# Last token block of a dense feed-forward stage: the down products of part 9 moved behind part 10 and accumulated with its own, tile by tile

## What is computed

```python
h = _layer_norm(x) * (1 + sc2) + sh2
a = jax.nn.silu(jnp.einsum('bsd,df->bsf', h, w_gate[l])) * jnp.einsum('bsd,df->bsf', h, w_up[l])
ffn = jnp.einsum('bsf,fd->bsd', a, w_down[l])
x = _layer_norm(ALPHA * x + (1 + g2) * ffn) * ln2_g[l] + ln2_b[l]
```

## Time and profile before

| what | value |
|---|---|
| median of 3 runs | 3033.78 us |
| span of the profiled execution | 3027.8 us |
| TensorE busy | 2900.4 us (96%) |
| VectorE busy | 2137.8 us (71%) |
| ScalarE busy | 1275.6 us (42%) |
| GpSimd busy | 1405.7 us (46%) |
| last matmul group ends | about 3005.2 us |
| last VectorE instruction begins | 3023.43 us |

### The profile page before, as it was taken

The page is one execution under the profiler, slowest core; times in us unless marked ns, Lnnn a source line. Parts: engine busy times, 40 slices in busy tenths (PEclk is TensorE's granted clock), DMA queues, the critical chain, the costliest instruction groups (busy, mean ns, idle before and its releaser), DMA issues.

```text
span 3027.8 us, 39376 instructions
## 1 busy us (share of the span) xinstructions
PE 2900.4 (96%) x14244; PEld 2438.3 (81%) x14244; DVE 2137.8 (71%) x3095; ACT 1275.6 (42%) x2287; POOL 1405.7 (46%) x1109
## 2 busy tenths in 40 slices
PE   7999998999999998999799999999999999999996
PEld 3888886666666656888789999989999989999995
DVE  5666665988888865566666666677777667777767
ACT  3111113777777764456533223343333333333334
POOL 0233321011111125568745545585677466676655
PEclk9999999999999998999999999999999999999998
DMA  7344337021312106366432122242332233322322
GB/s 260 120 140 133 121 121 191 28 70 58 84 58 72 50 22 213 121 214 212 170 125 70 56 84 70 84 157 77 119 112 82 86 109 132 118 86 103 112 70 91
DMA packets 194061, 333.02 MB, mean 110 GB/s; under 512 B 15366, under 2 KB 102599, under 8 KB 193866
## 3 DMA queue, kind: packets, MB, share of 16 engines
q1 hardware_dynamic: 193868, 330.49, 33.9%
HBM read 250.72 MB, written 79.71 MB: 109 GB/s over the span
## 4 chain that ended last, share of the span: by engine, by line
PE 51%; POOL 4%; DVE 3%; DVEq 1%; issue 1%; DMA 1%; POOLq 1%; ACT 1%; SPq 0%; ACTq 0%
PE tail_bank L2298 9%; PE tail_bank L2300 9%; PE tail_bank L2299 9%; PE tail_bank L2322 6%; PE tail_bank L2323 6%; PE tail_bank L2324 5%; PE tail_bank L2237 1%; PE tail_bank L2236 1%; PE tail_bank L2235 1%; POOL tail_rounded L2031 1%; POOL tail_rounded L2039 1%; DMA tail_plain<-scr_h_d 1%; PE tail_bank L2184 0%; POOL tail_plain L2027 0%; PE tail_bank L2176 0%
## 5 line engine op out<-in xcount | busy, mean ns | idle before, releaser
L2031 POOL TENSOR_TENSOR tail_rounded<-tail_plain,tail_rounded 128x512 fp32r<-128x512 f32 x462 | 648.4, 1425 | 491.0 <-ACT tail_rounded L1815 490.5
L2298 PE MATMUL tail_bank<-tail_rounded 128*128 128x384 f32 x1848 | 621.8, 336 | 18.9 <-POOL tail_rounded L2039 11.3
L2299 PE MATMUL tail_bank<-tail_rounded 128*128 128x384 f32 x1848 | 620.8, 336 | 0.0
L2300 PE MATMUL tail_bank<-tail_rounded 128*128 128x384 f32 x1848 | 620.6, 336 | 0.0
L2467 DVE TENSOR_TENSOR tail_plain<-tail_plain,tail_bank 128x384 f32<-128x384 f32 x462 | 247.9, 549 | 264.1 <-PE tail_bank L2300 198.5
L1815 ACT ACTIVATE tail_rounded<-tail_plain 128x512 fp32r<-128x512 f32 x462 | 271.4, 621 | 368.5 <-DVE tail_plain L2445 177.4
L2298 PEld LDWEIGHTS tail_bank<-tail_rounded 128*128 128x128 f32 x1848 | 348.6, 189 | 23.2 <-issue 17.0
L2299 PEld LDWEIGHTS tail_bank<-tail_rounded 128*128 128x128 f32 x1848 | 348.7, 189 | 1.3
L2300 PEld LDWEIGHTS tail_bank<-tail_rounded 128*128 128x128 f32 x1848 | 348.8, 189 | 0.0
L1154 DVE TENSOR_REDUCE att_peak<-att_sc 128x1 f32<-128x1024 f32 x256 | 312.7, 1222 | 42.5 <-PE att_sc L966 35.9
L2322 PE MATMUL tail_bank<-tail_rounded 128*128 128x512 f32 x792 | 311.8, 394 | 21.3 <-issue 7.1
(11 more groups left out here) (286 smaller groups left out, 5142.7 us busy)
## 6 DMA issues: line engine op xcount, KB each, us to landing
tail_plain<-in_w_gu SPq DMA_DIRECT2D x132, 512.0 KB, 4.9
keep_ahead<-in_w_dn SPq DMA_DIRECT2D x66, 512.0 KB, 6.6
proj_ada<-in_w_ada SPq DMA_DIRECT2D x16, 1024.0 KB, 6.8
held_w_hi<-scr_qs_d SPq DMA_DIRECT2D x128, 128.0 KB, 2.9
scr_h_d<-tail_plain SPq DMA_DIRECT2D x63, 256.0 KB, 4.5
tail_plain<-scr_h_d SPq DMA_DIRECT2D x45, 256.0 KB, 4.3
proj_x_in<-in_x SPq DMA_DIRECT2D x18, 512.0 KB, 6.4
scr_att_d<-held_w_hi SPq DMA_DIRECT2D x36, 256.0 KB, 2.9
```

The source lines that it names most:

```text
L2031: nc.gpsimd.tensor_tensor(w_lo[:, j, :], operand(F, j), w_hi[:, j, :].bitcast(F32), ALU.subtract).then_inc(wlo_done, 1)
L2298: nc.tensor.matmul(dst, w_hi[:, j, cols], h_hi[j][:, k, :], start=(k == 0), stop=False)
L2299: nc.tensor.matmul(dst, w_hi[:, j, cols], h_lo[j][:, k, :], start=False, stop=False)
L2300: m = nc.tensor.matmul(dst, w_lo[:, j, cols], h_hi[j][:, k, :], start=False, stop=(k == 3))
```

## The change

For the last part only (`END` = 32):

- TensorE: `down(31)` no longer stands between the two phases of part 32. Behind the second phase comes `last_two_downs`: the products of part 31 for the first four banks, then those of part 32 on top of them in the same banks; from the fifth bank on the products of both parts for one bank follow each other. VectorE reads each bank once, 12 reads instead of 24.
- Buffers: the activation and the down weights of part 32 go to the space of `h_hi[0]`, `h_lo[0]` and of `h_hi[1]`, `h_hi[2]`, `h_lo[1]`, `h_lo[2]`, since those of part 31 are still needed. So ScalarE's `split_down` and `split_a` wait for products of the second phase.
- `gate_sums` of tiles 0 to 3 goes from GpSimd to VectorE, between the two phases' takes, of tiles 4 and 5 it stays on GpSimd, but behind the four `split_a`.
- VectorE: `residual(0)` and `residual(1)` move ahead of and behind `take_u` of the second phase; both `split_down` move behind the first `multiply`; `residual(2)` comes after the last `multiply`, and `residual(n + 3)` and `finish(n - 1)` come inside the last loop.

```diff
+        last_a_hi, last_a_lo = (tile.rearrange("p (i c) t -> p i c t", c=2) for tile in (h_hi[0], h_lo[0]))
+        last_dn_hi, last_dn_lo = cut(11264, D, "i", i=2), cut(20480, D, "i", i=2)
...
             def split_down(G, i):
                 act.wait_ge(dnraw_landed[i], 16 * (G + 1))
-                if G:
+                if G == END:
+                    act.wait_ge(prod_done, OPERANDS * (2 * G + 1) + 3)
+                elif G:
                     act.wait_ge(dn_done, BANKS * G)
...
                 for j in range(OPERANDS):
+                    if j == 3 and is_last(b, part):
+                        split_down(G, 0)
+                        split_down(G, 1)
...
                 elif is_last(b, part):
-                    for n in range(TILES):
-                        gate_sums(G - 1, n)
                     for n in range(4):
                         split_a(G, n)
+                    for n in range(TILES - PT, TILES):
+                        gate_sums(n)
...
+            def last_two_downs():
+
+                for m_ in range(BANKS):
+                    if m_ == 0:
+                        pe.wait_ge(dnlo_done, 2 * END)
+                        pe.wait_ge(alo_done, 4 * END)
+                        for ahead_ in range(4):
+                            pe.wait_ge(added, BANKS * (END - 2) + BANKS - 3 + ahead_)
+                            down_products(END - 1, ahead_, True, False)
+                        pe.wait_ge(dnlo_done, 2 * END + 2)
+                        pe.wait_ge(alo_done, 4 * END + 2)
+                    if m_ == 4:
+                        pe.wait_ge(alo_done, 4 * END + 4)
+                    if m_ >= 4:
+                        pe.wait_ge(added, BANKS * (END - 1) + m_ - 3)
+                        down_products(END - 1, m_, True, False)
+                    down_products(END, m_, False, True).then_inc(dn_done, 1)
+
             def step(b, part, G):
                 phase(b, part, 2 * G)
                 if G == 0:
                     turn(NT - 2)
-                if part:
+                if part and G < END:
                     down(G - 1)
                 phase(b, part, 2 * G + 1)
-                if closes(part):
+                if G == END:
+                    last_two_downs()
+                elif closes(part):
                     down(G)
...
-                if part:
+                if is_last(b, part):
+                    last_sum_w(F + 1)
+                    for n in range(TILES - PT):
+                        gate_sums(total[:, DOWN_ORDER[n], :])
+                elif part:
                     down(b, part - 1, G - 1, beside_gate)
 
+                if is_last(b, part):
+                    residual(0)
                 take_u(F + 1, up)
                 if is_last(b, part):
-                    residual(2)
+                    residual(1)
                 elif G:
                     sums_w(F + 2)
-                if G:
+                if G and not is_last(b, part):
                     split_down(G, 0)
                 take_v(F + 1, up)
-                if closes(part):
+                if closes(part) and not is_last(b, part):
                     split_down(G, 1)
                 take_c11(F + 1, up)
                 multiply(G, 0)
                 if is_last(b, part):
-                    residual(3)
+                    split_down(G, 0)
+                    split_down(G, 1)
                 take_c21(F + 1, up)
...
             parts(step)
-            gate_last(0)
-            add_last(0)
-            gate_last(1)
-            residual(4)
-            add_last(1)
-            for n in range(2, TILES):
+            residual(2)
+            for n in range(TILES):
                 gate_last(n)
-                if n == 2:
-                    residual(5)
                 add_last(n)
-            for n in range(TILES):
-                finish(n)
+                if n < TILES - 3:
+                    residual(n + 3)
+                if n:
+                    finish(n - 1)
+            finish(TILES - 1)
```

More of the change, by code:

```diff
@@ L1453, in fourier_to_end, with a_of, dn_of @@
         LAST = NT - TILES
+        END = PARTS * BLOCKS - 1
+        def a_of(G):
+            return (last_a_hi, last_a_lo) if G == END else (a_hi, a_lo)
+        def dn_of(G):
+            return (last_dn_hi, last_dn_lo) if G == END else (dn_hi, dn_lo)
         def last_gate(n, half):
@@ L1853, in split_a @@
                 act.wait_ge(mult_done, 4 * G + n + 1)
-                if n == 0 and G:
+                if n == 0 and G == END:
+                    act.wait_ge(prod_done, OPERANDS * (2 * G + 1) + 1)
+                elif n == 0 and G:
                     act.wait_ge(dn_done, BANKS * G)
-                nc.scalar.activation(a_hi[:, i, c, :], sil[:, i, c, :], ACT.Copy).then_inc(ahi_done, 1)
+                nc.scalar.activation(a_of(G)[0][:, i, c, :], sil[:, i, c, :], ACT.Copy).then_inc(ahi_done, 1)
             def normalise(N, tile, at):
@@ L2043, in split_a @@
                 pool.wait_ge(ahi_done, 4 * G + n + 1)
-                nc.gpsimd.tensor_tensor(a_lo[:, i, c, :], sil[:, i, c, :], a_hi[:, i, c, :].bitcast(F32), ALU.subtract).then_inc(alo_done, 1)
+                hi, lo = a_of(G)
+                nc.gpsimd.tensor_tensor(lo[:, i, c, :], sil[:, i, c, :], hi[:, i, c, :].bitcast(F32), ALU.subtract).then_inc(alo_done, 1)
             def rstd(N, at):
@@ L2050, in rstd, with gate_sums @@
                 nc.gpsimd.tensor_tensor(at[:, 5:6], at[:, 4:5], at[:, 3:4], ALU.mult).then_inc(rstd_done, 1)
-            def gate_sums(G, n):
-                pool.wait_ge(added, BANKS * G + 2 * n + 2)
+            def gate_sums(n):
+                pool.wait_ge(added, BANKS * (END - 2) + 2 * n + 2)
                 if n == TILES - PT:
                     pool.wait_ge(row2_landed, 80)
[L2057 to L2060, removed]
+                for half in range(2):
+                    tile = total[:, DOWN_ORDER[n], half * 512:(half + 1) * 512]
+                    ins = nc.gpsimd.tensor_tensor(tile, tile, last_gate(n, half), ALU.mult)
                 ins.then_inc(gated, 1)
@@ L2317, in down @@
                         pe.wait_ge(added, BANKS * G + m_ - 3)
[L2318 to L2324, removed]
@@ L2325, in down, with down_products @@
-                    m.then_inc(dn_done, 1)
+                    down_products(G, m_, True, True).then_inc(dn_done, 1)
+            def down_products(G, m_, first, final):
+                pos, half = divmod(m_, 2)
+                q, c = divmod(DOWN_ORDER[pos], 2)
+                hi, lo = a_of(G)
+                w_hi, w_lo = dn_of(G)
+                dst = dn(m_)
+                tokens = slice(q * P, (q + 1) * P)
+                cols = slice(half * 512, (half + 1) * 512)
+                for i in range(2):
+                    nc.tensor.matmul(dst, hi[:, i, c, tokens], w_hi[:, i, cols], start=(first and i == 0), stop=False)
+                    nc.tensor.matmul(dst, hi[:, i, c, tokens], w_lo[:, i, cols], start=False, stop=False)
+                    m = nc.tensor.matmul(dst, lo[:, i, c, tokens], w_hi[:, i, cols], start=False, stop=(final and i == 1))
+                return m
@@ L2525, in gate_last @@
             def gate_last(n):
-                G = PARTS * BLOCKS - 1
                 if n == 0:
@@ L2532, in gate_last @@
                 for half in range(2):
-                    dve.wait_ge(dn_done, BANKS * G + 2 * n + half + 1)
+                    dve.wait_ge(dn_done, BANKS * (END - 1) + 2 * n + half + 1)
                     nc.vector.tensor_tensor(gated_dn(n)[:, half * 512:(half + 1) * 512], dn(2 * n + half),
@@ L2639, in beside_gate @@
                         late_norm(b, part, m)
-                    if is_last(b, part) and m in (8, 11):
-                        residual(m // 3 - 2)
                 def beside_up(m):
```

11 lines of the change are left out of this document (5 added, 6 removed).

## The result

The changed kernel takes 3037.52 us, the median of 17 runs (3034.90 to 3044.09). The kernel before, in the same study, takes 3031.18, again of 17 runs (3024.19 to 3035.36). The ratio is 1.0029, with a 95% interval from 1.0020 to 1.0037: slower by 6 to 11 us; the two medians lie 6.3 apart. The forecast was 3045.7 with a range from 3040 to 3050.

A forecast was written before the change was run, and what follows sets the result against it. TensorE was taken to bound the kernel until 3005.2, VectorE after it. The sixth add_last +18.1 us and what follows it -6.3 sum to +11.8; the span's +11.9 on 3033.78 gave 3045.7, range 3040 to 3050.

The forecast's parts named there:

- The base: Whole kernel: 3033.78 us, median of the runs shown, 6.0 above the profiled span; the predicted difference was added to it.
- The mechanism's own bounds: Whole kernel: +8.9 us with undisturbed turns to +15.4 with costlier rounds and later add_last(1); with run spread 3041 to 3050.5.
- the 11.9: Whole span: the changed kernel ends at 3039.7 against 3027.8 before, +11.9 us.
- Turns with GpSimd: Last part's second phase: VectorE and GpSimd SBUF instructions alternate whole, 1.13 and some 1.24 us each; add_last(1) ends at 2990.4.
- TensorE in the second phase: Last part: TensorE idles from 2953.8 to 2955.6, then waits 4.6 us for take_u; product 6 ends at 2974.4.
- The clock's price: Last part's second phase: half clock after TensorE's wait for take_u costs 1.6 us, bounds 0 and 1.6.
- The closed chain: Last loop: finish(n-1) waits for normalise(n-1), behind moments(n), which waits for add_last(n); 3.94 us a tile, rounds of 9.11; chance 88%.
- The end follows TensorE: Rival, last loop: finish(n-1) finds its tile normalised, so the kernel gets 3.0 to 6.0 us faster; chance 3%.
- The closed chain starts early: Rival, second phase: gate_sums and turns cost nothing, add_last(1) ends at 2981.1; +2.6 us, up to +6.0; chance 9%.
- without these waits the change would win: Last loop: without the closed chain's waits for ScalarE, 5 x 3.94 = 19.7 us, the change would be faster.

The follow-up runs named there:

- after_again: The changed kernel run once more with no edit: 3039.50 us, ratio 1.0042 to the kernel before.
- lag_two: The changed kernel with finish(n-2) instead of finish(n-1) in VectorE's last loop, finish(4) and finish(5) after it: 3020.39 us, ratio 0.9972 to the kernel before.
- early_gates: The changed kernel with VectorE's four gate_sums moved to gaps where VectorE waited for TensorE: ratio 1.0016 to the kernel before.
- before_again: The kernel before run once more with no edit: 3026.78 us, ratio 0.9999.
- act_order: The changed kernel with normalise(n-1) ahead of moments(n) in ScalarE's last loop: 3025.38 us, ratio 0.9995 to the kernel before.

## Why the prediction was right and wrong

**The base was wrong; this is the step that failed.** The prediction says: "The profiled execution's span is 6.0 us below the median of the runs shown (3033.78), which I leave as it is: 3045.7." The 6.0 were taken for a fixed distance between span and time. It is 1.8 in all eleven executions with both numbers on record. So the trace of before was, by these 1.8, that of an execution of 3029.6 us, and 3033.78 was the median of three draws, 2.6 above the median of 17 and 5.6 above that of 29 in the next study. Of the 8.2 us that the forecast was too high, 2.6 are this draw of the median; the other 5.6 are that the two medians of the first study lie 6.3 apart where the forecast, and the pair of traces, has 11.9 and 11.7. Trace plus 1.8 plus 11.9 gives 3041.5, and the profiled execution of the changed kernel took 3041.25; that these agree so well is partly luck, since the executions of one kernel spread from 3024 to 3035 before and from 3035 to 3044 after. The forecast added the difference of a trace to a median as if both came from the same execution, and its range had the spread of three runs in it, -2.2 to +1.6, and no more. (The mechanism's own bounds with this spread are 3040.5 to 3050.8, not the 3041 to 3050.5 written; that changes nothing.)

What an execution drew shows in its mean granted clock. Of the 29 executions of the kernel before in the next study, the nine with a clock of 0.982 or 0.983 took 3026.8 to 3034.8 us (median 3031.0), the fifteen with 0.985 to 0.987 took 3021.0 to 3031.0 (median 3023.9). The changed kernel's 17 go the same way: median 3040.9 for the eight up to 0.983, 3035.0 for the six from 0.985 on. Which of the two follows the other is not shown. The three runs that the forecast had came without their clocks.

**Was the 11.9 right?** As a difference of stages, yes: 11.4 and 11.6 between the pairs of traces. As a ratio, 1.0039 is just above the first study's interval (1.0020 to 1.0037) and inside the second's (1.0028 to 1.0056). The changed kernel's executions had a mean clock of 0.9838 in the first study and 0.9828 in the second; those of the kernel before have no clock on record in the first, so how much of the smaller ratio is such a draw stays open. The pair of traces of the first study has 11.7, so no trace shows a smaller mechanism behind the smaller ratio.

**Turns with GpSimd.** Right. The chain of instructions was off by less than a microsecond over 33 us: gate_sums end at 2966.6 (forecast 2966.8), residual(0) at 2967.8 (2968.0), take_u at 2968.2 (2968.55), add_last(1) at 2990.0 (2990.4).

**TensorE in the second phase.** Waits of 1.5 and 3.8 us were measured, forecast 1.8 and 4.6; the phase ended at 2974.1 by the switch to the down products, forecast 2974.4. The clock's price was not one number. The same 24 matmuls (products 5 and 6), after the same idle time of 3.80 us, in the table by stage of the changed kernel and of after_again (columns as in rows 2; the granted clock is 0.71 and 0.60 of full):

```profile
2968.40:2974.10 5.70, 5.70 (x24) 5.70 (x25) 5.51 (x6) 0.53 (x1) 1.37 (x1) 0.71 0.74 233
```
```profile
2963.80:2970.60 6.80, 6.77 (x25) 6.80 (x26) 6.43 (x8) 0.52 (x1) 1.37 (x1) 0.60 0.73 228
```

5.7 and 6.8 us, against 4.2 at full clock: the slow clock cost 1.5 and 2.6 us, where the forecast had 1.6 with bounds of 0 and 1.6. The 1.1 between the two reach the end: the second add_last ends 35.3 and 36.6 behind the split.

**The closed chain.** Right in mechanism and size. Waits of 2.80, 3.01, 3.93, 3.92 and 3.92 us (forecast 2.8 twice, 3.9 three times), 17.6 in all; rounds of 9.1 to 9.3; the last VectorE instruction ends 9.16 behind the sixth add_last (9.2). TensorE idled between tiles, once for 1.13 and once for 3.59 us, with a granted clock of 0.77 in that stage, and VectorE did not wait for it there.

**The rivals.** "The end follows TensorE" had 3%: the change would have had to leave the chain open. lag_two shows its worth: 0.9972 by the ratio (5 to 12 us below before), 5.2 and 6.2 us by the traces from the split; I gave it 3.0 to 6.0. "The closed chain starts early" is early_gates: I gave +2.6 to +6.0 us, and it measured +4.8 by the ratio.

**That without these waits the change would win** was put in one sentence and is only half right: with finish back behind the loop (finish_last) it is 1.0005. The gain needs both: finish in the gaps of VectorE, and far enough behind.

## What to carry to other kernels

When an instruction is moved forward in one engine's order, look at what stands ahead of its releaser in the other engine's order: two orders that were each harmless can close into a chain in which each waits for the other's newest tile. A consumer that lags by one more tile opened it here: one wait of 1.4 us was left of 17.6. And before adding a difference worked out from a trace to a median, find the time of the execution that was traced: here the span and 1.8 us, 4.2 below the median of three.

## What was not expected of the hardware

The last weights' transfer (two of 512 KB) did not always take the same time. From issue to landing the later of the two took 5.0 to 6.0 us in seven of the twelve traces and 8.1 to 8.7 in five, and GpSimd's idle time ahead of their first split was 6.1 to 7.1 us in those seven and 9.3 to 9.8 in those five. The kernel before has one trace of each kind (5.0 and 8.4), so an edit is not needed for it; the three traces with early gates are all of the first. What makes it late was not looked for. In before_again the whole 3.5 us of idle time reached the end although TensorE was busy when they began: the first phase had ended 3.7 us earlier than in the first trace, and the span was the same, 3027.8. TensorE idled longer ahead of its last down products (6.21 us for 4.19), so splits, gating and a_lo on GpSimd, not TensorE, set their start. And the same idle time of TensorE, 3.80 us, was followed by half clock for a different share of the same 24 matmuls in two executions of one kernel, as shown above (act_order, also after 3.80 us, has 6.9 us at a clock of 0.58): the price of a pause is a range, even where its length is known.
